# When the first FFN's weight sums are copied and added, and which engine rounds attention's first weights

## The chip, the cores and the metric

The kernel runs on one core of a Trainium2 chip. The time is the device time of one execution in microseconds (us). The engines are TensorE (PE in the profile; PEld is its weight load), VectorE (DVE), ScalarE (ACT), GpSimd (POOL) and SyncE (SP, which here only issues transfers). The core has 16 DMA engines; SP's transfers go through the queue that the profile calls hardware_dynamic (q1), GpSimd's through software_dynamic (q0).

## The reference

Two sequences, of 512 and 256 tokens with 16 learned tokens ahead of each (800 rows in all), go through a trunk of two layers: a bidirectional mLSTM mixer and a SwiGLU FFN, then differential attention and a SwiGLU FFN. All in float32.

```python
for i in range(DEPTH):                                   # DEPTH = 2
    xn = rmsnorm(h, norm_mix[i])
    h = h + (mlstm_mixer(xn, ...) if i % 2 == 0 else diff_attn(xn, ...))
    xn = rmsnorm(h, norm_ffn[i])
    gu = xn @ ffn_w_in[i]                                # 1024 -> 2 x 2816
    h = h + (silu(gu[..., :FF]) * gu[..., FF:]) @ ffn_w_out[i]
```

## The kernel before

**Float32 products.** TensorE multiplies rounded numbers. So each weight tile is loaded (`raw`, `raws`), rounded to a high part (`wh`, `w5h`), and the rest is taken as a low part (`wl`, `w5l`); a product is three matmuls per 128 rows of the weight: high by high, high by low, low by high.

**Blocks.** In the mixers a block is 128 output columns of a weight of 1024 rows: a tile of 512 KB, 48 matmuls (for 800 rows in two halves). Blocks are numbered: mLSTM's input projection has 24 (0 to 23), its output projection OUT0 = 24 to 31, attention's begin with MIX1 = 32. There are two slots. GpSimd's `split` (L715 to 727) does both steps: four casts (L722), four subtractions (L726). It waits until block n-1 is done, and SP's `weights` (L576) loads block n once split n-2 is done. Ahead of the output projection's third block SP also brings half of h back from DRAM (`h_kept`, L667).

**The FFN's jobs.** Each FFN is computed with seven products instead of eight (Strassen's scheme), so some factors are sums of weight quarters. An FFN has 42 jobs s: 22 are tiles of the first matrix ("input jobs", 12 matmuls per product), 20 of the second (6, in the last group 9). Each job has seven products j = 0 to 6, and `product_order` interleaves them into one list `ORDER` of 294 products, n = 0 to 293. Jobs 0 to 4, 9 to 12, 17 to 20 are input jobs; 5 to 8, 13 to 16 and so on are output jobs, run in between or alternating with an input job's products. The places of product 0 of some jobs: job 1 n = 7, 2 n = 14, 5 n = 33, 6 n = 38, 7 n = 46, 8 n = 53, 10 n = 70, 11 n = 77, 13 n = 89, 14 n = 94, 15 n = 102, 16 n = 109, 17 n = 115, 28 n = 196.

For each product n, SP loads the factor (`factor`, L603, DMA at L625: 256 KB for an input job, 128 KB for an output job), ScalarE rounds it (`high_part`, L2141 is its activation), GpSimd subtracts (`low_parts`, L756), TensorE multiplies (`product`, L922). There are seven raw buffers and five slots: load n waits for split n-7, rounding n waits for product n-5. All in program order on each engine; on ScalarE the rounding stands between copies of products (L2156), silu and roundings of the hidden factors.

**The weight sums.** The four sums of weight quarters that the scheme needs are made in DRAM by DMA. Each FFN's are cut into six parts of four copies and four adds, so there are 24 copies (`copy_for_sum`, L601, on SP's queue, 1280 or 1536 KB each) and 24 adds (`add_for_sum`, L738, L742, L748, accumulating transfers on GpSimd's queue, same sizes). An add waits for the copies of its part; the second kind of add waits for the first. Before the change, layer 0's copies 0 to 21 are issued with the blocks of mLSTM's input projection and 22, 23 with OUT0 and OUT0+1; its adds n-9 after split n for n = 9 to 31, and the last, add 23, in the FFN after split 14. Layer 1's copies are issued in the first FFN, one at product 0 of each of the jobs 10 to 33, its adds in attention.

Jobs 28 and up read the sums of layer 0's last two parts (copies and adds 16 to 23).

**From the FFN into attention.** The last products are 289 to 293. GpSimd then waits for product 290 (`prod_done` NF-3), splits block MIX1 (L722, L726), and TensorE's first attention block (L1329) follows product 293. Block MIX1's raw tile is loaded from 935 us on. ScalarE and VectorE meanwhile make `xh`, `xl` and squares of the last rows (L2282, L2285, L1542, L1549), then the root of the norm (L2126) and its reciprocal (L1422).

Of the kernel before, what the change touches and what calls it, by code (L numbers as in the profile page):

```python
# [21 lines left out]
F32 = mybir.dt.float32  # L22
F32R = mybir.dt.float32r
ALU = mybir.AluOpType
ACT = mybir.ActivationFunctionType
AX = mybir.AxisListType

P = 128
D = 1024
KT = D // P  # L30
# [4 lines left out]
KP = KT // 2  # L35
# [26 lines left out]
OUT0 = MIX0 + 6 * M_HEADS  # L62
MIX1 = OUT0 + KT
# [20 lines left out]
NPROD = 7  # L84
# [52 lines left out]
NF = len(ORDER)  # L137
# [31 lines left out]
N_SLOT, N_RAW = 5, 7  # L169
# [4 lines left out]
OUT_PARTS = ((0, 6), (6, 11))  # L174
PARTS = (("in", 0), ("in", 1), ("out", 0), ("in", 2), ("in", 3), ("out", 1))
N_PART = len(PARTS)


FX_POS = {B11: 1, T1: 2, B22: 3, T2: 4, T3: 5, B21: 6, T4: 7}
# [72 lines left out]
def trunk(nc, x_prompt, x_sample, meta_tokens, norm_mix, norm_ffn, m_w_in, m_b_gate, m_g_head, m_w_out,  # L252
# [3 lines left out]
    with ctx:  # L256
# [11 lines left out]
        raw = sb("raw", [P, 2, KT * P])  # L268
        wh, wl = sb("wh", [P, 2, KT * P], F32R), sb("wl", [P, 2, KT * P], F32R)
# [212 lines left out]
        raw_in = [sem("raw_in0"), sem("raw_in1")]  # L482
# [92 lines left out]
        def _(sp):  # L575
# [18 lines left out]
            def copy_for_sum(layer, i):  # L594

                part, which = divmod(i, 4)
                unit = N_PART * layer + part
                if which == 0 and unit > 1:
                    sp.wait_ge(sums_copied[unit % 2], 64 * (unit // 2))
                row, col = ((1, 0), (0, 0), (0, 0), (0, 1))[which]  # L600
                sp.dma_start(sum_columns(layer, (0, 2, 1, 3)[which], part),  # L601
                             weight_columns(layer, row, col, part)).then_inc(sums_copied[unit % 2], 16)
# [25 lines left out]
            def ffn_factors(layer):  # L628
                for n, (s, j) in enumerate(ORDER):
                    factor(layer, n)  # L630
                    if layer == 0 and j == 0 and 10 <= s < 34:
                        copy_for_sum(1, s - 10)

            def first_weights(j):
# [18 lines left out]
            for hd in range(1, M_HEADS):  # L653
                for j in range(6):
                    n = MIX0 + hd * 6 + j
                    weights(n, j % 2, mlstm_cols(hd, j))
                    if hd == 1 and j < 4:
                        copy_for_sum(0, 2 * j)
                        copy_for_sum(0, 2 * j + 1)
                    else:  # L660
                        copy_for_sum(0, n - 2)
            for j in range(2):
                weights(OUT0 + j, j, cols(m_w_out[0], j * P))
                copy_for_sum(0, OUT0 + j - 2)
            sp.wait_ge(pv_done, M_HEADS * NT)
            sp.wait_ge(h_stored, 16)
            sp.dma_start(h[:, KP:KT, :], h_kept).then_inc(h_back, 16)  # L667
# [29 lines left out]
        def _(pool):  # L697
# [18 lines left out]
            def split(n, slot, times, wait=True, k=KT):  # L716
                if wait:
                    pool.wait_ge(block_done, n - 1)
                pool.wait_ge(raw_in[slot], 16 * times)
                pool.sem_inc(pool_passed, 1)  # L720
                for c in pieces(k * P):
                    ins = pool.tensor_copy(wh[:, slot, c], raw[:, slot, c])  # L722
                ins.then_inc(w_hi, 1)
                pool.wait_ge(w_hi, n + 1)
                for c in pieces(k * P):
                    ins = pool.tensor_tensor(wl[:, slot, c], raw[:, slot, c], wh[:, slot, c].bitcast(F32), ALU.subtract)  # L726
                ins.then_inc(w_split, 1)


            def add_for_sum(layer, i):  # L730

                pair, step = divmod(i, 8)
                part = 2 * pair + ((step // 2) if step < 4 else step % 2)
                unit = N_PART * layer + part
                if step < 4:
                    pool.wait_ge(sums_copied[unit % 2], 64 * (unit // 2 + 1))
                    which, other = ((0, weight_columns(layer, 1, 1, part)), (2, weight_columns(layer, 1, 0, part)))[step % 2]
                    pool.dma_start(sum_columns(layer, which, part), other,  # L738
                                   accum_op=ALU.add).then_inc(sums_added[unit % 2], 16)
                elif step < 6:  # L740
                    pool.wait_ge(sums_added[unit % 2], 32 * (unit // 2 + 1))
                    pool.dma_start(sum_columns(layer, 1, part), sum_columns(layer, 0, part),  # L742
                                   accum_op=ALU.add).then_inc(sums_second[unit % 2], 16)
                else:
                    pool.wait_ge(sums_second[unit % 2], 16 * (unit // 2 + 1))
                    if unit > 1:
                        pool.wait_ge(sums_fourth[unit % 2], 16 * (unit // 2))
                    pool.dma_start(sum_columns(layer, 3, part), sum_columns(layer, 1, part),  # L748
                                   accum_op=ALU.add).then_inc(sums_fourth[unit % 2], 16)

            def low_parts(layer):
                for n, (s, j) in enumerate(ORDER):
                    pool.wait_ge(prod_hi, NF * layer + n + 1)
                    columns = k_tiles_of(s) * P
                    for c in pieces(columns):
                        ins = pool.tensor_tensor(slot_of(n, 1)[:, c], raw_of(n)[:, c], slot_of(n, 0)[:, c].bitcast(F32),  # L756
                                                 ALU.subtract)
                    ins.then_inc(prod_split, 1)
                    if layer == 0 and n == 2 * NPROD:
                        add_for_sum(0, 23)  # L760

            split(0, 0, 1, wait=False)
            pool.wait_ge(xl_ready, KT - 1)
            split(1, 1, 1, wait=False)
            for n in range(2, MIX1):
                split(n, n % 2, n // 2 + 1)
                if n >= 9:
                    add_for_sum(0, n - 9)
            low_parts(0)
            def split_rest(q):  # L770

# [10 lines left out]
                ins.then_inc(w_split, 1)  # L782

            pool.wait_ge(prod_done, NF - 3)
            split(MIX1, 0, MIX1 // 2 + 1)
            for x in (at[:, :, :, :], va[:, :, :, :]):
                pool.memset(x, 0.0).then_inc(attn_zeroed, 1)
            pool.wait_ge(prod_done, NF)
# [1327 lines left out]
        def _(sc):  # L2116
# [176 lines left out]
            def ffn(layer):  # L2293
                w, f0 = WIDTH[layer], layer * FT

                def silu(f):
                    gate = gate_up(layer, f)[0]
                    sc.wait_ge(g_ready, f0 + f + 1)
                    sc.activation(gate[:, 0:2 * w], gate[:, 0:2 * w], ACT.Silu).then_inc(silu_ready, 1)

                copied, finished = 0, 0
                for n in range(3, NF):
                    s, j = ORDER[n]
                    f = TILE_OF.get(s)
                    if f is not None and j < 3:
                        product_copy(layer, f, j)
                    if n + N_SLOT < NF:
                        high_part(layer, n + N_SLOT)
                    if n == 5:
                        root(2 * layer + 2)  # L2310
                    if f == 1:
                        if j == 0:
                            silu(0)
                        elif j < 3:
                            high_of_pair(layer, 0, (B11, T1)[j - 1])
                    elif f and f % 2 and j < 2:
                        high_of_pair(layer, f // 2, (B11, T1)[j])
                    elif f and f % 2 == 0 and j < 3:
                        for which in ((B22, T2), (T3, B21), (T4,))[j]:
                            high_of_pair(layer, f // 2 - 1, which)  # L2320
                    if f and j == 5:
                        silu(f)
                    if f == FT - 1 and j == 6:
                        for which in (B22, T2, T3, B21, T4):
                            high_of_pair(layer, f // 2, which)
                        if layer == 0:
                            rope_loads()
                    if layer == 0 and finished < KT and PLACE[LAST_TILES[finished]] + 1 <= n:
                        high_and_square(finished)
                        finished += 1  # L2330
                    while layer == 1 and copied < len(LAST_HALVES) and PLACE[LAST_HALVES[copied]] + 3 <= n:
                        copy_result(copied)
                        copied += 1
                if layer == 0:
                    lambda_loads()
                    for i in range(finished, KT):
                        high_and_square(i)
                    sc.wait_ge(lam_sums, 2)
                    sc.activation(lam[:, 4:6], lam[:, 0:2], ACT.Exp).then_inc(lam_exp, 1)
                    root(3)  # L2340
                else:
                    for t in range(copied, len(LAST_HALVES)):
                        copy_result(t)
# [292 lines left out]
```

## Time and profile before

| | |
|---|---|
| median of 3 runs | 1909.01 us (1906.89 to 1911.67) |
| the profiled execution | 1908.87 us, span 1907.0 us, mean granted clock 0.998 |
| TensorE busy | 1880.2 us (99% of the span) |
| VectorE, ScalarE, GpSimd busy | 65%, 46%, 61% |
| DMA | 305.39 MB, mean 160 GB/s; q1 40.6%, q0 20.0% of the 16 engines' span |
| chain that ended last | TensorE 89%, VectorE 6%, DMA 2% |

The span is the time from the first to the last instruction; the time of the runs has about 2 us around it. Times inside it are counted from its start. Stages: mLSTM's input projection and cells to 359 us, its output projection to 440, the first FFN to 948, attention to about 1417, the second FFN to the end. The granted clock is TensorE's, as a share of 2.4 GHz.

### The profile page before, as it was taken

How to read it: one execution, taken by the hardware profiler on the slowest of the kernel's cores; microseconds unless marked ns; L12 is line 12 of the kernel's file. 1: busy time of each engine (PE TensorE's matmuls, PEld its weight loads, DVE VectorE, ACT ScalarE, POOL GpSimd, SP SyncE). 2: the span in 40 equal slices, each digit the busy share in tenths (PEclk: the TensorE clock that was granted, in tenths of full speed). 3: DMA queues.
4: the chain of work that ended last, by engine and by line, in shares of the span. 5: the costliest groups of instructions: out<-in, count | busy, mean ns of one | idle time of the engine just before them, and what ended most of it. 6: DMA issues, size and time to landing. Idle time of an engine off the chain costs nothing.

```text
span 1907.0 us, 31586 instructions
## 1 busy us (share of the span) xinstructions
PE 1880.2 (99%) x10881; PEld 1750.9 (92%) x10881; DVE 1241.4 (65%) x2148; ACT 870.1 (46%) x1837; POOL 1165.7 (61%) x1537
## 2 busy tenths in 40 slices
PE   8999999999999999999999999999999999999999
PEld 7888887899999999999988888888889999999998
DVE  7756465667757565656776666666488575756673
ACT  6333333335544444445524444444465454544453
POOL 4533524376877777788853333333358787887885
PEclk9999999999999999999999999999999999999999
DMA  5559999697466978763366666656124435353534
GB/s 164 183 194 258 231 257 240 172 198 171 114 204 214 281 219 273 225 184 108 113 137 127 128 122 125 126 116 117 57 84 122 133 111 150 97 153 103 153 115 129
DMA packets 378985, 305.39 MB, mean 160 GB/s; under 512 B 14259, under 2 KB 322262, under 8 KB 378598
## 3 DMA queue, kind: packets, MB, share of 16 engines
q1 hardware_dynamic: 348304, 233.69, 40.6%
q0 software_dynamic: 28416, 69.21, 20.0%
q8 instruction: 73, 1.20, 0.3%
q10 hardware_dynamic: 2134, 0.82, 0.2%
q14 instruction: 58, 0.48, 0.1%
HBM read 298.88 MB, written 143.20 MB: 232 GB/s over the span
## 4 chain that ended last, share of the span: by engine, by line
PE 89%; DVE 6%; DMA 2%; ACT 1%; issue 1%; POOL 1%; ACTq 0%; DVEq 0%; SPq 0%; POOLq 0%
PE ps L922 50%; PE ps L829 24%; PE ps L1075 3%; PE ps L1236 3%; PE ps L1204 2%; DMA raw<-in_m_w_out_dram 2%; PE ps L1055 1%; PE ps L1226 1%; PE ps L1138 1%; POOL wl L726 1%; DVE rstd L1422 1%; DVE sx L1474 0%; PE ps L1168 0%; PE ps L1329 0%; PE ps L1040 0%
## 5 line engine op out<-in xcount | busy, mean ns | idle before, releaser
L922 PE MATMUL ps<-sx,wh 128*128 128x400 f32 (+1 forms) x2044 | 530.3, 340 | 0.9 <-POOL wl L756 0.5
L756 POOL TENSOR_TENSOR wl<-raw,wh 128x256 fp32r<-128x256 f32 (+1 forms) x432 | 352.5, 840 | 100.1 <-ACT wh L2141 98.7
L722 POOL CAST wh<-raw 128x256 fp32r<-128x256 f32 x252 | 105.2, 465 | 492.4 <-PE ps L829 443.8
L922 PEld LDWEIGHTS ps<-sx,wh 128*128 128x128 f32 x2044 | 373.4, 188 | 2.7 <-ACT gt_first L2156 0.9
L922 PE MATMUL ps<-sx,wl 128*128 128x400 f32 (+1 forms) x1022 | 347.6, 340 | 0.0
L756 POOL TENSOR_TENSOR wl<-raws,wh 128x256 fp32r<-128x256 f32 x328 | 285.2, 890 | 85.8 <-ACT wh L2141 84.8
L1633 DVE TENSOR_TENSOR h<-h,ps 128x400 f32<-128x400 f32 (+1 forms) x280 | 154.6, 559 | 132.5 <-PE ps L922 132.4
L922 PE MATMUL ps<-fx,wh 128*128 128x400 f32 (+1 forms) x904 | 235.3, 341 | 0.1
L829 PE MATMUL ps<-xh,wh 128*128 128x512 f32 (+1 forms) x752 | 215.9, 363 | 0.0
L829 PE MATMUL ps<-xl,wh 128*128 128x512 f32 (+1 forms) x752 | 207.4, 349 | 0.0
L726 POOL TENSOR_TENSOR wl<-raw,wh 128x256 fp32r<-128x256 f32 x252 | 198.9, 817 | 5.2
L829 PE MATMUL ps<-xh,wl 128*128 128x512 f32 (+1 forms) x752 | 201.3, 345 | 0.0
L922 PEld LDWEIGHTS ps<-sx,wl 128*128 128x128 f32 x1022 | 191.9, 188 | 0.0
L2141 ACT ACTIVATE wh<-raw 128x512 fp32r<-128x512 f32 (+2 forms) x268 | 142.4, 535 | 101.2 <-PE ps L922 93.2
L2141 ACT ACTIVATE wh<-raws 128x512 fp32r<-128x512 f32 (+2 forms) x202 | 108.5, 537 | 163.8 <-PE ps L922 155.8
L922 PEld LDWEIGHTS ps<-fx,wh 128*128 128x128 f32 x904 | 164.6, 188 | 0.5 <-issue 0.5
L922 PE MATMUL ps<-fx,wl 128*128 128x400 f32 (+1 forms) x452 | 153.7, 340 | 0.0
L922 PE MATMUL ps<-sx,w5h 128*128 128x400 f32 (+1 forms) x532 | 138.4, 341 | 0.3 <-ACT gt L2156 0.3
L829 PEld LDWEIGHTS ps<-xh,wh 128*128 128x128 f32 x752 | 120.8, 189 | 18.4 <-issue 7.4
L829 PEld LDWEIGHTS ps<-xl,wh 128*128 128x128 f32 x752 | 126.2, 188 | 10.5
L829 PEld LDWEIGHTS ps<-xh,wl 128*128 128x128 f32 x752 | 124.5, 188 | 10.8
L756 POOL TENSOR_TENSOR w5l<-raw,w5h 128x256 fp32r<-128x256 f32 x112 | 92.4, 841 | 21.7 <-ACT w5h L2141 21.5
(309 smaller groups left out, 3588.4 us busy)
## 6 DMA issues: line engine op xcount, KB each, us to landing
in_sums<-in_ffn_w_in_dram SPq DMA_DIRECT2D x16, 1536.0 KB, 9.2
raw<-in_sums SPq DMA_DIRECT2D x96, 256.0 KB, 3.0
in_sums<-in_ffn_w_in_dram SPq DMA_DIRECT2D x16, 1280.0 KB, 8.2
raw<-in_ffn_w_in_dram SPq DMA_DIRECT2D x80, 256.0 KB, 3.0
raws<-in_sums SPq DMA_DIRECT2D x80, 256.0 KB, 3.0
raw<-out_sums SPq DMA_DIRECT2D x120, 128.0 KB, 2.4
raws<-in_ffn_w_in_dram SPq DMA_DIRECT2D x52, 256.0 KB, 3.1
raw<-in_m_w_in_dram SPq DMA_DIRECT2D x24, 512.0 KB, 4.6
```

The costliest lines, as they stand in the source:

```text
L722: ins = pool.tensor_copy(wh[:, slot, c], raw[:, slot, c])
L726: ins = pool.tensor_tensor(wl[:, slot, c], raw[:, slot, c], wh[:, slot, c].bitcast(F32), ALU.subtract)
L756: ins = pool.tensor_tensor(slot_of(n, 1)[:, c], raw_of(n)[:, c], slot_of(n, 0)[:, c].bitcast(F32), ALU.subtract)
L829: mm = pe.matmul(out, w[:, slot, k * P:(k + 1) * P], x[:, k, a:b], start=(k + q == 0), stop=(k == k_tiles - 1 and q == 2), skip_group_chec ...
L922: mm = pe.matmul(product_bank(layer, s, j), slot_of(n, low_w)[:, k * P:(k + 1) * P], x, start=(j in OPENS and k + q == 0), stop=(k == tile ...
L1055: mm = pe.matmul(flat(2 + 0)[0:tz, (j % 2) * 1024 + a:(j % 2) * 1024 + b], wk[:, 1, t0:t0 + tz], wk[:, 0, START[s] + a:START[s] + b], star ...
L1075: mm = pe.matmul(ps[0:tz, 4 + 2 * (i % 2) + d, 0:M_DV + 2], w, v, start=(j == js[0] and t == 0), stop=(j == js[-1] and t == 2), skip_group ...
L1138: mm = pe.matmul(square_sums[0:lhs.shape[1], 2 * i:2 * i + 2], lhs, cst[:, COMP:COMP + 2], start=True, stop=True, skip_group_check=True)
L1204: return pe.matmul(both[:, c, a:b], wk[rows, odd, i * P:(i + 1) * P], wk[rows, 2 + odd, START[s] + a:START[s] + b], start=True, stop=True)
L1236: mm = pe.matmul(acc_o, at[:, i % 2, q, :], va[:, odd, j, :], start=(q == 0), stop=(j == js[-1]), skip_group_check=True)
L1633: ve.tensor_tensor(part, part, product_bank(layer, s, j), ALU.add if result_of(s, j)[0] >= 4 else ALU.subtract).then_inc(out_read, 1)
L2141: sc.activation(slot_of(n, 0)[:, 0:columns], raw_of(n)[:, 0:columns], ACT.Copy).then_inc(prod_hi, 1)
```

## The change

Layer 0's copies 16 to 23 are no longer issued with blocks 18 to 25 but in the first FFN, at product 0 of the jobs 1 to 8. Its adds 16 to 23 are no longer issued after splits 25 to 31 and in the FFN after split 14, but in the FFN after the split of product 0 of the jobs 6, 7, 10, 11, 13, 14, 16 and 17. Add 15 stays after split 24.

ScalarE makes the high part of block MIX1: one half after product 289, the other after product 290, in its own order of the FFN's work. GpSimd no longer casts there: it waits for both halves and subtracts. It also no longer waits for the raw tile or for an earlier block itself.

```diff
+LATE_ADDS = (6, 7, 10, 11, 13, 14, 16, 17)
...
                 for n, (s, j) in enumerate(ORDER):
                     factor(layer, n)
-                    if layer == 0 and j == 0 and 10 <= s < 34:
+                    if layer == 0 and j == 0 and 1 <= s < 9:
+                        copy_for_sum(0, s + 15)
+                    elif layer == 0 and j == 0 and 10 <= s < 34:
                         copy_for_sum(1, s - 10)
...
-                    else:
+                    elif n < 18:
                         copy_for_sum(0, n - 2)
             for j in range(2):
                 weights(OUT0 + j, j, cols(m_w_out[0], j * P))
-                copy_for_sum(0, OUT0 + j - 2)
...
                     ins.then_inc(prod_split, 1)
-                    if layer == 0 and n == 2 * NPROD:
-                        add_for_sum(0, 23)
+                    if layer == 0 and j == 0 and s in LATE_ADDS:
+                        add_for_sum(0, 16 + LATE_ADDS.index(s))
...
-                if n >= 9:
+                if 9 <= n < 25:
                     add_for_sum(0, n - 9)
...
             pool.wait_ge(prod_done, NF - 3)
-            split(MIX1, 0, MIX1 // 2 + 1)
+            pool.wait_ge(w_hi, MIX1 + 1)
+            for c in pieces(KT * P):
+                ins = pool.tensor_tensor(wl[:, 0, c], raw[:, 0, c], wh[:, 0, c].bitcast(F32), ALU.subtract)
+            ins.then_inc(w_split, 1)
...
                     if n + N_SLOT < NF:
                         high_part(layer, n + N_SLOT)
+                    elif layer == 0 and n >= NF - N_SLOT and n < NF - N_SLOT + 2:
+                        part = slice(KP * P, KT * P) if n == NF - N_SLOT else slice(0, KP * P)
+                        sc.wait_ge(prod_done, n + 1)
+                        sc.wait_ge(raw_in[0], 16 * (MIX1 // 2 + 1))
+                        ins = sc.activation(wh[:, 0, part], raw[:, 0, part], ACT.Copy)
+                        if n > NF - N_SLOT:
+                            ins.then_inc(w_hi, 1)
```

## Rows read from the trace of the kernel before

**Rows 1.** The chain that ended last, whole span: start us, us, what.

```profile
359.41 16.11 DMA raw<-in_m_w_out_dram
...
397.46 13.39 DMA raw<-in_m_w_out_dram
...
486.15 456.94 PE ps L922 x2505
```

**Rows 2.** TensorE in order, 355 to 417: start us, us, operation, [idle before <-releaser].

```profile
381.32 0.63 PE L829 MATMUL ps<-yh,wh 128*128 128x400 f32 x2 [1.84 <-POOL wl L726]
...
411.67 0.62 PE L829 MATMUL ps<-yh,wh 128*128 128x400 f32 x2 [2.23 <-POOL wl L726]
```

**Rows 3.** Busy time by engine (PE, PEld, DVE, ACT, POOL), clock, DMA share, GB/s.

```profile
381.00:386.00 5.00, 4.68 (x17) 4.69 (x18) 4.46 (x4) 2.43 (x5) 4.92 (x9) 0.66 0.73 167
```

**Rows 4.** DMA issues of 387.8 to 388.2: queue, count, KB each, us to landing.

```profile
out_sums<-in_ffn_w_out_dram POOLq DMA_DIRECT2D x1, 1280.0 KB, 15.2
raw<-in_m_w_out_dram SPq DMA_DIRECT2D x1, 512.0 KB, 17.7
```

**Rows 5.** DMA issues of 381.0 to 381.5.

```profile
raw<-in_m_w_out_dram SPq DMA_DIRECT2D x1, 512.0 KB, 4.2
```

**Rows 6.** DMA issues of 359 to 360.

```profile
h<-h_kept SPq DMA_DIRECT2D x1, 1600.0 KB, 7.7
```

**Rows 7.** All engines in order, 940 to 962.

```profile
943.28 1.92 POOL L722 CAST wh<-raw 128x256 fp32r<-128x256 f32 x4 [1.69 <-PE ps L922]
...
945.24 1.62 DVE L1542 SCALAR_TENSOR_TENSOR xl<-h,par,xh 128x800 fp32r<-128x800 f32 x1
...
945.27 4.30 POOL L726 TENSOR_TENSOR wl<-raw,wh 128x256 fp32r<-128x256 f32 x4
...
949.63 0.63 PE L1329 MATMUL ps<-xh,wh 128*128 128x400 f32 x2 [1.62 <-POOL wl L726]
...
959.88 0.15 DVE L1536 TENSOR_SCALAR lam<-lam 128x1 f32<-128x1 f32 x1
...
960.99 5.15 DVE L1422 RECIPROCAL rstd<-rstd 128x800 f32<-128x800 f32 x1 [0.95 <-ACT rstd L2126]
```

**Rows 8.** The first FFN's matmuls (L922): PE, PEld busy (count), clock, DMA share, GB/s.

```profile
439.60:640.00 200.40, 198.96 (x1084) 197.32 (x1085) 1.00 0.64 185
```

**Rows 9.** SP, GpSimd and TensorE in order, 516 to 534.

```profile
516.15 3.64 SPq L625 DMA_DIRECT2D raws<-in_ffn_w_out_dram  x3
516.48 0.74 POOL L756 TENSOR_TENSOR wl<-raws,wh 128x256 fp32r<-128x256 f32 x1 [0.36 <-ACT wh L2141]
...
522.30 3.54 SPq L625 DMA_DIRECT2D raw<-out_sums  x4
...
528.49 0.74 POOL L756 TENSOR_TENSOR wl<-raw,wh 128x256 fp32r<-128x256 f32 x1 [0.35 <-ACT wh L2141]
...
532.16 0.53 PE L922 MATMUL ps<-fx,wh 128*128 128x400 f32 x2
```

**Rows 10.** DMA issues of 621.3 to 621.6.

```profile
in_sums<-in_ffn_w_in_dram SPq DMA_DIRECT2D x1, 1536.0 KB, 7.5
raw<-out_sums SPq DMA_DIRECT2D x1, 128.0 KB, 7.2
```

**Rows 11.** Busy time by engine as in Rows 3, in the first FFN.

```profile
600.00:660.00 60.00, 60.00 (x331) 60.00 (x330) 33.95 (x53) 26.20 (x56) 43.42 (x55) 1.00 0.90 279
```

**Rows 12.** DMA queues in 434 to 440, an add beside loads: packets, MB, share.

```profile
q0 software_dynamic: 356, 1.09, 93.5%
q1 hardware_dynamic: 358, 0.18, 15.2%
```

**Rows 13.** The same in 280 to 288, an add beside a copy.

```profile
q1 hardware_dynamic: 393, 1.21, 41.4%
```

**Rows 14.** DMA issues of 192.7 to 193.4, issued beside an add.

```profile
in_sums<-in_ffn_w_in_dram SPq DMA_DIRECT2D x1, 1280.0 KB, 13.9
```

**Rows 15.** SP in order, 608 to 630.

```profile
627.62 0.98 SPq L625 DMA_DIRECT2D raws<-in_ffn_w_out_dram  x1
```

## The prediction

> **What bounds the kernel now.** I read the page first, then the chain that ended last, then the stretch around each place that the change touches. On the page TensorE is busy for nearly the whole span, so time can come only from the few places where it idles, and a new place where it idles costs in full. The chain [rows 1] shows both kinds. In the mLSTM's output projection it runs twice through a transfer, `raw<-in_m_w_out_dram`, 16.11 and 13.39 us. In the first FFN it is one piece of 2505 matmuls, 456.94 us, with nothing between: there TensorE waits for nobody.
>
> A chain piece of 16.11 us is not a gap of 16.11 us. In the order of TensorE's instructions [rows 2] it idles 1.84 us ahead of block OUT0+2 (381.32) and 2.23 us ahead of OUT0+5 (411.67), both times for GpSimd's split, which waited for the load. Behind the first gap the granted clock is 0.66 over 5 us [rows 3]: TensorE works part of it at the lower level (1.2 GHz) after it idled, which costs (1 - 0.66) x 5 = 1.7 us. I take the same behind the second. So late loads cost the projection 1.84 + 2.23 + 2 x 1.65 = 7.4 us.
>
> Why they are late: the 512 KB load for OUT0+5 took 17.7 us while an add of GpSimd's queue (15.2 us) flew [rows 4]; one issued together with an add, whose packets had not begun, took 4.2 [rows 5].
>
> **The change, part by part.**
>
> *Output projection.* Adds 16 to 22 leave the seven splits from OUT0+1 on, copies 16 to 23 leave SP's queue in head 3 and at OUT0 and OUT0+1. What is left beside the weights is the reload of h, 7.7 us [rows 6], with the load of OUT0+2 behind it: together at most 7.7 + 4.2 = 12 us from 359.4, so it lands by 371.4 and is split by 377 (5.5 us as in the old rows), before TensorE wants it at 379.5. Both gaps and both slow stretches go: -7.4 us. Bounds: 0 to -7.4, for behind each gap stand only TensorE's own matmuls; I take the whole, since the adds are gone altogether. GpSimd also issues seven DMAs fewer between splits (no gain, it waits for TensorE there). What follows up to 486 us hangs on TensorE, ScalarE and VectorE and slides forward whole.
>
> *ScalarE's rounding.* At the FFN's end GpSimd starts four casts at 943.28, when product 290 is done, and four subtractions at 945.27 that take 4.30 us; TensorE waits 1.62 us, until 949.63 [rows 7]. In the new kernel ScalarE rounds one half after product 289 and the other after 290, ahead of the xh copy that stands there. A rounding takes about half a us (my estimate; GpSimd's four casts took 1.92), so the xh copy moves by about 1 us, and VectorE's operation that reads it starts only at 945.24 [rows 7]: nobody behind it is late. The subtractions start at about 943.8, 1.5 us earlier, and end at 948.1 at the latest; TensorE comes at 948.0. Its gap goes. But VectorE's reciprocal, the chain's next piece (960.99), stands behind VectorE's small operations, the last of which ends at 960.03 [rows 7]: it can move by 0.95 us and no more. I take -0.9 (bounds 0 and -1.6).
>
> *First FFN: what comes in.* Eight copies (jobs 1 to 8) and eight adds (jobs 6, 7, 10, 11, 13, 14, 16, 17, at product 0 of each) instead of the one add at product 14. Each product's factor is loaded, rounded by ScalarE, split by GpSimd, and SP issues load n+7 when split n ends. So the question is how long a load may take. TensorE is 1084 matmuls into the FFN at 640.0 [rows 8], at 331 in 60 us; product 47 (job 6, factor 4) has 492 ahead of it, so it is the one that starts at 532.16 [rows 9]. Its load is the first of the four issued from 522.30, its split runs from 528.49 to 529.23 [rows 9], behind 0.5 us of ScalarE. A load there may take 532.16 - 522.30 - 1.35 = 8.5 us before TensorE stands. Where a copy stands ahead of a load in SP's queue, the load takes 7.2 us already (copy 7.5) [rows 10]: the copies that are there now use nearly all of the slack, and TensorE loses nothing. The way from load to product is nine products of 6 matmuls. Where products have 12, in the input jobs, it is 9 x 2.18 = 19.6 us, less 2.2 for the longer split: 17 us.
>
> The eight copies alone I cost at 0: same sizes, same place in the queue as those from job 10 on, under which TensorE is busy 60.00 us of 60 at a DMA share of 0.90 [rows 11]. From above, one late load each in jobs 5 to 8: 2 us.
>
> The adds are another matter. While an add flies, the two queues move packet for packet: 356 and 358 beside loads in 6 us [rows 12], 60 per us; beside a copy 393 in 8 us [rows 13], 49 per us. A copy beside an add took 13.9 us [rows 14]. An add or copy is 512 packets of 2.5 or 3 KB, or 640 of 2 KB; a 128 KB load is 256 of 512 B. A copy alone moves about 150 per us (from its 7.5 us, less some 3.5 of start and end: an estimate).
>
> The Trainium skill says the same (DMA: Bandwidth & Descriptors, "Queues, rings and completion order"): each DMA engine takes the queues that have work in turn, one packet of each. By that rule a load's small packets go at the pace of the add's large ones; if the engines were shared by bytes, the loads would lose only half their rate and the sum would be rival 1's. The trace agrees with turn-taking (356 to 358).
>
> Three places, in the times of the profiled run:
> - A, jobs 6 and 7. Split 38 (516.48) ends at 517.2, its add's packets flow from about 520. Load 46, the third of those from 516.15 [rows 9], takes till 524.3. Copy 22 (640 packets, behind it) moves 226 beside the rest of the add, to 529, 300 alone until the next add, issued just ahead of split 47, flows at 531, and the last 114 beside that, to 533.2. Load 47 needs 256 / 60 = 4.3 us more and lands at 537.8, split at 539.1; TensorE has waited since 532.2: **7 us**.
> - B, jobs 13 to 15, two adds 9 us apart. Products of 12 and of 6 matmuls alternate, so the way is half as long again as in A, and only one copy falls in: **3 us**, an estimate between 0 and A's.
> - C, jobs 16 and 17. Add 22 is issued with load 116 (627.62 [rows 15]), the copy of layer 1 just ahead of them. That copy takes 512 / 49 = 10.4 us from 630.4, to 641; load 116 lands at 642, load 117 (512 packets) goes beside add 23 at 80 per us (2 KB packets), to 648. Product 117 has 1086 matmuls ahead, so it starts at 640.4 and wants its load by 638: **10 us**.
>
> The adds at jobs 10 and 11 meet input jobs alone, 14 us of latency where 17 are free: 0. Behind each of the three waits TensorE works at the lower clock: 3 x 1.65 = 5. Sum 25 us. Bounds: below, 0 if the waits don't come; above, about 45 if ScalarE, held by a late load, also brings its product copies and silu late, so that banks come free late. GpSimd's own waits in the adds are met long before, and the first job that reads these sums is the 28th.
>
> **Sum.** -7.4 - 0.9 + 25 = +16.7 us. The profiled execution took 1908.87 us (span 1907.0); the median is 1909.01, 0.01% above. Forecast: 1926 us.
>
> **Rivals.**
> 1. The FFN absorbs it. For: with copies alone it loses nothing, and four products are split ahead. Against: A comes to 537.8 - 522.3 = 15.5 us of latency where 8.5 are free, and the projection shows 17.7 [rows 4]. 1908.9 - 8.3 = 1900.6. Chance 0.18.
> 2. Only one of the places bites and cancels the gain: 1904 to 1912. Chance 0.10.
> 3. Heavier: each late load holds ScalarE's queue, five or six waits come, each with its slow clock. For: ScalarE rounds in order, with product copies behind. Against: it is busy only 26.20 of 60 us [rows 11] and catches up. 1908.9 - 8.3 + 45 = 1946. Chance 0.19.
> 4. The reload of h alone keeps the projection's first gap: 3.7 us less gain, 1930. Chance 0.05.
>
> The sign turns where a load behind a copy and beside an add takes more than about 8.5 us.
>
> **Chances.** Forecast 0.48. Over 0.3% (6 us) is what a measurement of this kernel can tell from no change. Faster: 0.18 of rival 1 and 0.01 of 2, 0.19. Same: 0.06, of rival 2. Slower: 0.75, the rest. Range 1900 to 1944: down to rival 1, without the upper half of rival 3. The forecast's own range is 1918 to 1938.
>
> **What would show it.** No `raw<-in_m_w_out_dram` in the chain and no granted clock under 1 in the output projection; TensorE no longer idle ahead of L1329's first matmul. In the first FFN, idle stretches of TensorE for GpSimd's split with a load behind it near products 47, 98 to 103 and 116 to 117, a lower clock after them, and ScalarE waiting for a DMA over 5 us at a time. If TensorE is busy 60 of 60 us through jobs 5 to 18, the packet-for-packet reckoning of late loads failed, and the forecast with it.

## The result, and the profile after

The changed kernel takes 1933.22 us (median of 4 runs, 1931.89 to 1934.96), the kernel before, in the same session, 1910.34 us (4 runs, 1906.89 to 1913.50): ratio 1.0121, 95% interval 1.0107 to 1.0135. It is 23 us slower. The profiled execution took 1933.13 us, its span is 1931.3 and its mean granted clock 0.991, where the kernel before had 1907.0 and 0.998. Ratios, here and below, are of the mean times; medians are given beside them.

Line numbers are 4 to 7 higher in the new kernel: the FFN's matmuls are L929, GpSimd's low part L760, ScalarE's high part L2148 and, for MIX1, L2320, the mixers' blocks L836 and L1336, a split's casts L726 and subtractions L730, VectorE's reciprocal L1429.

Chain of waits, whole span (start us, us, what):

```profile
375.75 3.83 POOL wl L730 x4
379.71 52.90 PE ps L836 x288
...
514.11 11.23 DMA raw<-out_sums
526.68 12.84 DMA raw<-out_sums
...
582.74 13.86 DMA raw<-in_sums
...
621.35 13.12 DMA raw<-out_sums
635.82 5.54 DMA raw<-out_sums
642.71 19.69 DMA raw<-in_sums
664.74 270.37 PE ps L929 x1470
```

This stands against [rows 1]. The two transfers are gone from the output projection, which is one piece of 288 matmuls; the one piece in the first FFN is broken by transfers of weights down to 664.74.

TensorE's instructions in order, against [rows 2]: the only one in the output projection (360 to 432) that came after idle time, then all those between 520 and 670:

```profile
379.71 0.63 PE L836 MATMUL ps<-yh,wh 128*128 128x400 f32 x2 [0.19 <-POOL wl L730]
...
526.79 1.00 PE L929 MATMUL ps<-fx,wh 128*128 128x400 f32 x2 [2.67 <-POOL wl L760]
540.97 1.00 PE L929 MATMUL ps<-fx,wh 128*128 128x400 f32 x2 [4.98 <-POOL wl L760]
615.43 0.63 PE L929 MATMUL ps<-sx,wh 128*128 128x400 f32 x2 [0.58 <-DVE ut L1573]
623.33 0.60 PE L929 MATMUL ps<-fx,wh 128*128 128x400 f32 x2 [1.09 <-POOL wl L760]
626.57 0.60 PE L929 MATMUL ps<-fx,wh 128*128 128x400 f32 x2 [1.90 <-POOL wl L760]
629.84 1.00 PE L929 MATMUL ps<-fx,wh 128*128 128x400 f32 x2 [1.95 <-POOL wl L760]
657.44 1.01 PE L929 MATMUL ps<-fx,w5h 128*128 128x400 f32 x2 [5.13 <-POOL w5l L760]
664.74 1.01 PE L929 MATMUL ps<-sx,wh 128*128 128x400 f32 x2 [4.96 <-POOL wl L760]
```

The first row is the start of the projection's third block, where [rows 2] has 1.84 us; the stop of 2.23 us has no successor. The other eight are products 47, 54, 92, 97, 98, 99, 116 and 117: 23.3 us. Seven of them wait for GpSimd's split; the one of 0.58 us, product 92, waits for VectorE (`ut`).

Busy time by engine, clock, DMA share, GB/s, first in the stretch of [rows 3], then behind the second and last waits:

```profile
381.00:386.00 5.00, 5.00 (x29) 5.00 (x28) 4.06 (x5) 2.84 (x5) 4.13 (x5) 1.00 0.33 97
...
540.00:545.00 5.00, 4.03 (x12) 4.03 (x13) 0.57 (x1) 2.28 (x6) 4.42 (x7) 0.50 0.73 201
...
664.00:669.00 5.00, 4.26 (x13) 4.25 (x14) 0.93 (x2) 2.69 (x6) 3.34 (x5) 0.50 0.83 236
```

The output projection runs at the full clock. In the first FFN the granted clock falls to 0.50, the level of 1.2 GHz, behind the second and the last wait, and stays there for the whole of each stretch.

The FFN's matmuls from the first to the last, TensorE's busy time and then its weight loads', before (L922) and after (L929):

```profile
439.69:947.84 508.15, 506.79 (x2772) 504.72 (x2772) 1.00 0.65 192
```

```profile
432.45:974.78 542.33, 517.72 (x2772) 513.59 (x2772) 0.97 0.76 217
```

These two rows are the ledger. The FFN begins 439.69 - 432.45 = 7.24 us earlier and takes 34.18 us longer: idle time went from 1.36 to 24.61 us (+23.25), and the same 2772 matmuls are busy 10.93 us longer, at the lower clock. From the FFN's last matmul to the end of the span it takes 2.64 us less (959.16 to 956.52). 34.18 - 7.24 - 2.64 = +24.30, the difference of the spans.

How long the loads take is seen in the DMA issues of 514 to 519 and of 642.6 to 644.2 (queue, count, KB each, median us to landing), where the load of [rows 5] took 4.2 and that of [rows 10] 7.2:

```profile
raw<-out_sums SPq DMA_DIRECT2D x4, 128.0 KB, 10.0
```

```profile
raw<-in_sums SPq DMA_DIRECT2D x2, 256.0 KB, 20.9
raw<-out_sums SPq DMA_DIRECT2D x1, 128.0 KB, 22.1
```

And the two queues' packets, MB and share in 530 to 535, where an add flies (q0) beside a copy (q1), as in [rows 13]:

```profile
q0 software_dynamic: 245, 0.75, 77.2%
q1 hardware_dynamic: 245, 0.49, 29.3%
```

Packet for packet to the last one, 49 per us each, as in [rows 13]; beside loads [rows 12] showed 356 to 358.

At the FFN's end, all engines in order:

```profile
968.81 0.62 ACT L2320 ACTIVATE wh<-raw 128x512 fp32r<-128x512 f32 x1
...
970.05 0.63 ACT L2320 ACTIVATE wh<-raw 128x512 fp32r<-128x512 f32 x1 [0.62 <-PE ps L929]
...
970.83 3.59 POOL L791 TENSOR_TENSOR wl<-raw,wh 128x256 fp32r<-128x256 f32 x4 [2.30 <-ACT wh L2320]
...
974.78 0.53 PE L1336 MATMUL ps<-xh,wh 128*128 128x400 f32 x2
...
981.13 0.35 DVE L1535 CUSTOM_DVE_ANT_0 lv<-lv 128x64 f32<-128x64 f32 x1
...
986.06 5.15 DVE L1429 RECIPROCAL rstd<-rstd 128x800 f32<-128x800 f32 x1 [0.44 <-ACT rstd L2133]
```

L791 is the subtraction that the change writes out. It ends at 974.42, ahead of TensorE's need, and the idle 1.62 us of [rows 7] is gone.

### The profile page after: what moved, and what is told of

It reads as the page before. It is cut to its first block, busy times and chain, and to the rows that moved or that the text cites. A ratio compares the mean times of both kernels' runs of the same rounds, so it can differ in the third digit from the quotient of the medians.

```text
span 1931.3 us, 31585 instructions
## 1 busy us (share of the span) xinstructions
PE 1887.1 (98%) x10881; PEld 1756.6 (91%) x10881; DVE 1246.1 (65%) x2148; ACT 871.4 (45%) x1839; POOL 1161.5 (60%) x1533
## 4 chain that ended last, share of the span: by engine, by line
PE 85%; DVE 5%; DMA 4%; POOL 2%; ACT 2%; issue 1%; SPq 0%; ACTq 0%; DVEq 0%; POOLq 0%
PE ps L929 45%; PE ps L836 25%; PE ps L1082 3%; PE ps L1243 3%; PE ps L1211 2%; DMA raw<-out_sums 2%; DMA raw<-in_sums 2%; PE ps L1062 1%; POOL wl L760 1%; PE ps L1233 1%; PE ps L1145 1%; DVE rstd L1429 1%; PE ps L1091 1%; DVE sx L1481 0%; PE ps L1175 0%
## 5 line engine op out<-in xcount | busy, mean ns | idle before, releaser
L929 PE MATMUL ps<-sx,wh 128*128 128x400 f32 (+1 forms) x2044 | 531.7, 341 | 6.2 <-POOL wl L760 5.5
L760 POOL TENSOR_TENSOR wl<-raw,wh 128x256 fp32r<-128x256 f32 (+1 forms) x432 | 352.2, 842 | 123.5 <-ACT wh L2148 122.1
L726 POOL CAST wh<-raw 128x256 fp32r<-128x256 f32 x248 | 102.2, 454 | 488.9 <-PE ps L836 466.1
L929 PEld LDWEIGHTS ps<-sx,wh 128*128 128x128 f32 x2044 | 374.5, 188 | 8.0 <-issue 5.5
L929 PE MATMUL ps<-sx,wl 128*128 128x400 f32 (+1 forms) x1022 | 348.3, 341 | 0.0
L760 POOL TENSOR_TENSOR wl<-raws,wh 128x256 fp32r<-128x256 f32 x328 | 284.2, 895 | 81.7 <-ACT wh L2148 81.3
L929 PE MATMUL ps<-fx,wh 128*128 128x400 f32 (+1 forms) x904 | 239.9, 347 | 12.9 <-POOL wl L760 12.6
L836 PE MATMUL ps<-xh,wh 128*128 128x512 f32 (+1 forms) x752 | 215.5, 363 | 0.0
L836 PE MATMUL ps<-xl,wh 128*128 128x512 f32 (+1 forms) x752 | 207.4, 349 | 0.0
L2148 ACT ACTIVATE wh<-raw 128x512 fp32r<-128x512 f32 (+2 forms) x268 | 142.5, 535 | 132.0 <-PE ps L929 88.8
L836 PE MATMUL ps<-xh,wl 128*128 128x512 f32 (+1 forms) x752 | 201.3, 345 | 0.0
L730 POOL TENSOR_TENSOR wl<-raw,wh 128x256 fp32r<-128x256 f32 x248 | 196.7, 822 | 5.1
L929 PEld LDWEIGHTS ps<-sx,wl 128*128 128x128 f32 x1022 | 192.5, 188 | 0.0
L2148 ACT ACTIVATE wh<-raws 128x512 fp32r<-128x512 f32 (+2 forms) x202 | 108.5, 538 | 163.0 <-PE ps L929 150.5
L929 PEld LDWEIGHTS ps<-fx,wh 128*128 128x128 f32 x904 | 167.5, 192 | 15.1 <-issue 13.6
L929 PE MATMUL ps<-fx,wl 128*128 128x400 f32 (+1 forms) x452 | 155.6, 344 | 0.0
L929 PE MATMUL ps<-sx,w5h 128*128 128x400 f32 (+1 forms) x532 | 138.3, 341 | 0.3 <-ACT gt L2163 0.3
L836 PEld LDWEIGHTS ps<-xh,wh 128*128 128x128 f32 x752 | 120.8, 189 | 18.6 <-issue 7.4
L836 PEld LDWEIGHTS ps<-xl,wh 128*128 128x128 f32 x752 | 126.2, 188 | 10.3
L836 PEld LDWEIGHTS ps<-xh,wl 128*128 128x128 f32 x752 | 124.4, 188 | 10.8
L760 POOL TENSOR_TENSOR w5l<-raw,w5h 128x256 fp32r<-128x256 f32 x112 | 93.5, 856 | 22.9 <-ACT w5h L2148 22.7
## 6 DMA issues: line engine op xcount, KB each, us to landing
in_sums<-in_ffn_w_in_dram SPq DMA_DIRECT2D x16, 1280.0 KB, 10.3
```

Of the source, the lines that this page charges most:

```text
L836: mm = pe.matmul(out, w[:, slot, k * P:(k + 1) * P], x[:, k, a:b], start=(k + q == 0), stop=(k == k_tiles - 1 and q == 2), skip_group_chec ...
L929: mm = pe.matmul(product_bank(layer, s, j), slot_of(n, low_w)[:, k * P:(k + 1) * P], x, start=(j in OPENS and k + q == 0), stop=(k == tile ...
L2148: sc.activation(slot_of(n, 0)[:, 0:columns], raw_of(n)[:, 0:columns], ACT.Copy).then_inc(prod_hi, 1)
```

## The experiments

Each kernel is compared with the kernel before on the same chip and in the same session. The reference's median was 1910.34 beside the changed kernel and 1910.44, 1911.43 or 1910.82 in the three sessions below, so the sessions agree within 1.1 us.

**The rounding alone.** The kernel before with ScalarE's rounding of MIX1 and nothing else of the change.

```diff
-            split(MIX1, 0, MIX1 // 2 + 1)
+            pool.wait_ge(w_hi, MIX1 + 1)
+            (GpSimd's four subtractions, ScalarE's two roundings as in the change)
```

> The kernel before with ScalarE's rounding of attention's first block and nothing else. Forecast's step: TensorE's gap of 1.62 us ahead of L1329's first matmul goes, VectorE's reciprocal moves by 0.95 us at most: -0.9 us. Rival (the reciprocal moves the whole way, since VectorE's small operations slide too): -1.6 us. Rival (the rounding holds ScalarE's xh copy and the gap only changes hands): 0.

1906.04 us against 1910.44; ratio 0.9983 (0.9972 to 0.9994): by the ratio 3.2 us faster, between 1.1 and 5.3, by the medians 4.4. In the profile TensorE's wait ahead of its first attention block fell from 1.62 to 0.37 us, and the way from the FFN's end to the reciprocal from 13.15 to 11.92. That is 1.2 us, between the 0.9 of the forecast and the 1.6 of the first rival. Where the rest of the 3.2 comes from is not shown; the profiled execution was one of the slower (1908.93). It does show how executions of this program differ. The projection's second stop took 0.43 us instead of 2.23 and the FFN began 3.46 us earlier (436.23), and then TensorE stopped there, where the kernel before had no stop, with the granted clock at 0.66 behind it (443 to 448):

```profile
443.86 1.03 PE L925 MATMUL ps<-sx,wh 128*128 128x400 f32 x2 [3.10 <-ACT gt_first L2159]
```

ScalarE had waited 3.46 us for a weight load beside which an add flew.

**The adds' transfers cut away.** The changed kernel, with layer 0's adds 16 to 23 reduced to 16 columns of one row block. The kernel leaves the sums of the last two parts unfinished, so only its time is of use.

```diff
+                def cut(x):
+                    return x[:, 0:1, 0:16] if layer == 0 and i >= 16 else x
-                pool.dma_start(sum_columns(...), other, ...)
+                pool.dma_start(cut(sum_columns(...)), cut(other), ...)
```

> The kernel after, with layer 0's adds 16 to 23 cut to one 128-row tile by 16 columns each (so the last two parts' sums are left unfinished); all copies, waits and places as in the kernel after. Theory (the adds cost everything, the eight copies nothing): TensorE has no gap in the first FFN from product 20 on, and the gains of the output projection and of the rounding stay: 1901 us, -8 against before, -32 against after. Rival (the copies of jobs 5 to 8 are late by themselves): gaps at products 47 and 54 stay, 1906 to 1909 us.

1898.31 us (1897.82 to 1898.76); ratio to the kernel before 0.9938 (0.9919 to 0.9958). Its FFN, read as above:

```profile
432.65:939.85 507.20, 506.06 (x2772) 504.92 (x2772) 1.00 0.69 209
```

All eight waits and all the slow clock are gone, with the eight copies where the change put them. So the adds' transfers cost 1933.2 - 1898.3 = 34.9 us, and the copies by themselves nothing. It is also the price of everything else in the change: -12.1 us against its own reference, 1910.44, by the ratio between -8.0 and -15.5. The forecast had -8.3. The profiled executions differ by 10.3 (spans 1907.0 and 1896.7): 7.0 up to the FFN's start, 1.0 in the FFN, 2.3 behind it.

**One add, with and without a copy.** The kernel before, its add 23 moved from product 14 to product 46 (job 7, where no copy is near), and in a second kernel to product 109 (job 16, beside layer 1's copies).

```diff
-                    if layer == 0 and n == 2 * NPROD:
+                    if layer == 0 and (s, j) == (7, 0):      # second kernel: (16, 0)
                         add_for_sum(0, 23)
```

> The kernel before, with add 23 (640 packets of 2 KB) issued behind the split of product 46 (job 7, products of 6 matmuls) instead of product 14. No copy is in SP's queue there. Theory (loads and adds go packet for packet, and a load is late only where a copy stands ahead of it too): the add moves its packets for about 8 us, loads issued in it take 4 to 7 us where 8.5 are free, TensorE stays busy, 0 +- 2 us against before. Rival (any add among output jobs stalls TensorE, with or without a copy): a gap of 3 to 5 us near products 51 to 56 and a slow clock behind it, +5 us.

> The kernel before, with the same add 23 issued behind the split of product 109 (job 16), where one of layer 1's copies is issued at the same moment. Theory (copy and add share packet for packet, the copy takes 10 us instead of 4, the load behind it is late): TensorE idles 3 to 5 us at product 116 and works at the lower clock behind it, +5 us (4 to 7) against before. Rival (an add alone is what hurts): the same loss as in the kernel with the add at job 7. Rival (an add hurts only with a second add behind it): 0.

Job 7: 1910.19 us, ratio 0.9999 (0.9987 to 1.0011). Job 16: 1916.85 us, ratio 1.0036 (1.0023 to 1.0049). TensorE's stops in the first, and in the second:

```profile
538.71 0.60 PE L922 MATMUL ps<-fx,wh 128*128 128x400 f32 x2 [0.93 <-POOL wl L756]
```

```profile
641.95 1.00 PE L922 MATMUL ps<-fx,w5h 128*128 128x400 f32 x2 [3.29 <-POOL w5l L756]
645.52 1.00 PE L922 MATMUL ps<-sx,wh 128*128 128x400 f32 x2 [1.23 <-POOL wl L756]
```

The same transfer costs nothing in one place and 6.4 us in the other. The issues behind them, job 7 (525.8 to 530), then job 16 (628.9 to 630.4):

```profile
out_sums<-out_sums POOLq DMA_DIRECT2D x1, 1280.0 KB, 12.0
raw<-out_sums SPq DMA_DIRECT2D x3, 128.0 KB, 9.2
```

```profile
raw<-in_sums SPq DMA_DIRECT2D x2, 256.0 KB, 14.2
raw<-out_sums SPq DMA_DIRECT2D x1, 128.0 KB, 13.9
```

9.2 us is just over the 8.5 that the prediction gave an output job's load before TensorE stands, and the stop is just under 1 us. With a copy in front it is 14. The two kernels differ in more than the copy: two of the loads at job 16 are of 256 KB. One add at job 16 without layer 1's copies was not run; the copies alone are taken away further on, from the changed kernel.

**The copies back.** The changed kernel, copies 16 to 23 back beside blocks 18 to 25; adds as changed.

```diff
-                    if layer == 0 and j == 0 and 1 <= s < 9:
-                        copy_for_sum(0, s + 15)
...
+                copy_for_sum(0, OUT0 + j - 2)
```

> The kernel after, with layer 0's copies 16 to 23 back in head 3 and at OUT0 and OUT0+1; the adds stay at jobs 6 to 17. Theory (a load is late only behind a copy beside an add): at jobs 6 to 8 no copy is left, so the gaps at products 47 and 54 shrink from 8 us to at most 2 and their slow clock goes; those at jobs 12 to 17 stay, where layer 1's copies stand. 1923 us (1920 to 1926), -10 against after. Rival (adds one job apart are enough): 1931 to 1934.

1925.03 us, ratio 1.0073 (1.0055 to 1.0092), in the range that I expected. Place A, jobs 6 and 7, shrinks from 2.67 + 4.98 to one stop of 2.28 us at full clock, and the output projection still ends as early (FFN at 432.43): the adds were what delayed it, not the copies. B (products 99 and 100) has 1.91 + 1.21, and C is larger, 13.3 us against 10.1:

```profile
650.73 1.01 PE L928 MATMUL ps<-fx,w5h 128*128 128x400 f32 x2 [10.20 <-POOL w5l L759]
656.19 1.00 PE L928 MATMUL ps<-sx,wh 128*128 128x400 f32 x2 [3.12 <-POOL wl L759]
```

**Layer 1's copies later.** The changed kernel; the copies that fall beside B and C begin at job 18.

```diff
-                    elif layer == 0 and j == 0 and 10 <= s < 34:
-                        copy_for_sum(1, s - 10)
+                    elif layer == 0 and j == 0 and 18 <= s < 42:
+                        copy_for_sum(1, s - 18)
```

> The kernel after, with layer 1's 24 copies at jobs 18 to 41 instead of 10 to 33, so that no copy stands beside the adds of jobs 10 to 17. Theory: the gaps at 92 to 101 go; of those at 116 and 117 (10.6 us) some 5 us stay, since two adds follow each other there and load 117 is 512 packets long; those at 47 and 54 stay. 1922 us (1918 to 1926). Rival (the adds alone do it): 1931 to 1934.

1917.48 us, ratio 1.0030 (1.0019 to 1.0042), just below the range that I expected. A stays (2.19 and 6.02 us), B is gone, and C is down from 10.1 us to 1.84 + 2.15 (products 117 and 119). This is the cleanest evidence for the copy's part: the adds are the same and in the same places. It also shows that the copy is not all of it. Two adds that follow each other among output jobs still cost 4.0 us at C with no copy near, and 2.3 at A in the kernel above.

**The adds in input jobs.** The changed kernel; its adds at input jobs, where the prediction counted 17 us free.

```diff
-LATE_ADDS = (6, 7, 10, 11, 13, 14, 16, 17)
+LATE_ADDS = (10, 11, 12, 18, 19, 25, 26, 27)
```

> The kernel after, with the eight adds at jobs 10, 11, 12, 18, 19, 25, 26 and 27 (input jobs, products of 12 matmuls), copies as in the kernel after. Theory (a load may take 17 us there, beside a copy and an add it takes 14 to 16): most gaps go, 2 to 5 us stay where the products turn to 6 matmuls behind job 12. 1904 us (1900 to 1908), faster than before. Rival (each add costs what it cost, 4 us, wherever it is): 1931 us.

1911.14 us, ratio 1.0001 (0.9990 to 1.0013). 22 us back against the changed kernel, but 7 short of what I expected, which was a kernel faster than before; it is level with it. Two stops are left, 3.88 us at product 88 and 3.27 at product 186, and they are of another kind. TensorE's waits (engine, line, waited for: us, times, longest), TensorE's and ScalarE's order at the first of them:

```profile
PE ps L929 <- ACT gt L2163: 7.4, 3, 3.9
```

```profile
598.66 0.63 ACT L2148 ACTIVATE wh<-raw 128x512 fp32r<-128x512 f32 x1 [4.92 <-DMA raw<-in_sums]
...
600.04 0.48 ACT L2163 ACTIVATE gt<-ps 128x400 f32<-128x400 f32 x1
```

```profile
600.58 1.03 PE L929 MATMUL ps<-sx,wh 128*128 128x400 f32 x2 [3.88 <-ACT gt L2163]
```

TensorE has its weights. It waits for a bank, which ScalarE empties (L2163), and ScalarE stood 4.92 us in front of a rounding whose load took 13.3 us. The bound on a load is here where ScalarE's program meets it, not where TensorE needs it: 13.3 - 3.9 = 9.4 us were free, an estimate from this one stop. This is the mechanism of rival 3, at a small part of its price. It does not strike at every such load: in the changed kernel the load issued at 582.74, at job 12, took 13.9 us,

```profile
raw<-in_sums SPq DMA_DIRECT2D x1, 256.0 KB, 13.9
```

ScalarE waited 4.82 us for it, and TensorE did not stop: the next copy of a product in ScalarE's order (L2163, at 601.77) had itself to wait 1.35 us for TensorE.

**Adds and copies apart.** Both together: `LATE_ADDS = (4, 9, 10, 11, 12, 17, 18, 19)`, and layer 1's copies from job 18.

> The kernel after, with the adds at jobs 4, 9, 10, 11, 12, 17, 18 and 19 and layer 1's copies at jobs 18 to 41, so that adds and copies hardly meet. Theory: no gap in the first FFN from product 20 on; the output projection's and the rounding's gains are kept, 1899 us (1897 to 1902), as with the adds cut short. Rival (24 bytes-heavy adds anywhere in the FFN cost some us each): over 1905.

1903.08 us (1901.01 to 1907.90), ratio 0.9952 (0.9935 to 0.9968): faster than both kernels, 4 us above what I expected. The profiled execution is the slowest of the four (1907.90), so its stops are more than the median's. At jobs 10 to 12, where no copy flies, it has one stop of 1.11 us, again for ScalarE's L2163; at 17 to 19, where copies of layer 1 fly again from job 18 on, three of 1.05, 0.94 and 2.53 us.

**No add beside a copy.** Copies 16 to 23 as before the change, adds in the first input jobs, layer 1's copies from job 18.

```diff
+LATE_ADDS = (1, 2, 3, 4, 9, 10, 11, 12)
```

> The changed kernel with three places moved: layer 0's copies 16 to 23 back beside blocks 18 to 25 and the output projection's first two, its adds 16 to 23 at product 0 of jobs 1, 2, 3, 4, 9, 10, 11 and 12 (all input jobs), layer 1's copies from job 18 on. So in the first FFN no add flies beside any copy. If a load is late only where a copy stands ahead of it and an add beside it (my theory), no gap of TensorE follows any of the eight adds but for at most 1 us each at jobs 9 to 12, where output jobs' last loads or two products in turn are near, and the time is near that with the adds cut away: 1899 us, 1897 to 1903. Rival: an add beside 256 KB loads alone costs too, since a load of 512 packets at 60 to 80 per us takes 7 to 9 us and ScalarE's queue is held, as adds_and_copies_apart showed at product 72 (1.3 us): then 1903 to 1908, with gaps behind each of the adds.

1901.40 us (7 runs, 1901.00 to 1902.56), ratio 0.9960 (0.9945 to 0.9974). Its FFN:

```profile
432.50:942.86 510.36, 507.82 (x2772) 504.25 (x2772) 1.00 0.75 209
```

This is inside the 1897 to 1903 that I expected. Eight whole adds in the first FFN cost 3 us here (1901.4 against 1898.3 with the adds cut away), where the change paid 34.9, and the granted clock is 1.00 over the FFN. Of the rival's gaps behind each add only one is near its size, 0.96 us at product 72. Three things differ from the changed kernel at once: no copy is near an add, the adds stand at input jobs, and most of them are further apart. How the 32 us divide among the three is not shown. GpSimd's time for issuing an add, 1.2 to 1.5 us, is paid here too, so it is not by itself what stopped TensorE. Like the kernel before it in this section it beats both the old and the changed one; the intervals of the two overlap, so neither is shown to be the better.

## Why the prediction was right

The forecast was 1926 us and slower; it is 1933.2, inside the forecast's own range of 1918 to 1938. The mechanism held in all three places: loads behind a copy and beside an add came late, and ScalarE waited for transfers up to 6.2 us at a time. The sizes within a place held less well.

- **Output projection, -7.4.** -7.24, and nothing idles over 0.2 us in it. Rival 4 (the reload of h keeps the first gap) is out: the reload took 6.7 us and the load of OUT0+2, forecast by 371.4, landed at 369.1.
- **ScalarE's rounding, -0.9.** TensorE's gap went, as forecast. The cap did not hold: I took VectorE's small operations to end 0.95 us ahead of the reciprocal whatever happens, but the first of them had waited 1.73 us for its own transfer in the old trace (`lv`, at 955.62), and no longer does. From the FFN's end to the reciprocal it takes 1.87 us less, to the end of the span 2.64; the last 0.8 is not traced. The forecast took a wait for a load as fixed work.
- **The eight copies, 0.** Shown by the kernel with the adds cut away.
- **Add beside copy.** A was forecast at 7 us and took 7.7, B at 3 (0.6 + 1.1 + 1.9 + 2.0 = 5.5), C at 10 (10.1): 20 forecast, 23.3 measured. Moving layer 1's copies took away B and most of C, moving layer 0's most of A, and the two kernels with one add agree; what stays without a copy, 2.3 to 4.0 us, was seen only where two adds follow each other. That A came out so close is in part luck. The forecast had load 47 take 15.5 us and product 47 wait 7; the load took 11.2 and the product waited 2.67. The other 4.98 us are at product 54, whose load took 12.8 us and which the forecast left out. B was an estimate between 0 and A's, and 0.58 of its 5.5 us waits for VectorE, not for a split.
- **Slow clock, 5.** The term that was mis-sized: 10.9. I counted three waits, there were five long enough to be followed by the level of 1.2 GHz (2.67, 4.98, 1.95, 5.13, 4.96), and 10.9 / 5 is 2.2 us for each, not 1.65. This one term, 5.9 us too small, is most of the 7 us between forecast and result; the waits add 3.3, and the 1.7 more that was gained behind the FFN goes the other way.
- **Adds at jobs 10 and 11, 0.** Right: 14 us of latency were forecast and 13.9 measured, with no stop. But the 17 us of slack in input jobs do not hold everywhere. The kernel with its adds in input jobs stopped TensorE for 3.88 us behind a load of 13.3, because ScalarE's order came into it.
- **Turn-taking.** 245 to 245 packets in 5 us. The 80 per us that the forecast took for an add of 2 KB packets show as 243 in 3 us in the kernel with the add at job 7. What the reckoning lacked is the start: a load issued while an add flies moves nothing at first. In the kernel with the add at job 7, the first of four loads is issued at 528.11, and in 528 to 531 the queues show:

```profile
q0 software_dynamic: 208, 0.43, 98.9%
```

and there is no row for q1. From 532 to 535 the two are level again, 243 and 223. These 3 us are a large part of why a load beside an add alone takes 9.2 us and not the 256 / 60 = 4.3 of its packets.

Rival 1 (absorbed) had nearly the right time for the change without its adds, 1900.6 against 1898.3, but the adds were not absorbed. Rival 3's five or six late loads came, seven of them by the stops, but not its cause: each of the changed kernel's seven large stops waits for GpSimd's split, a late operand, and none for a bank.

## What to carry to other kernels

A background transfer costs by what flies beside it and by the slack where it flies: the same eight adds cost 34.9 us in one placement and 3 in another. Look for the places where an accumulating transfer of one queue meets a large copy standing ahead of small loads in the other, or a second add right behind it, and keep them apart before giving up either. Read the slack of a load at the first engine whose program order meets it, here ScalarE, and at what stands behind it there, not at the engine that finally needs the data. And when a forecast has waits of TensorE in it, price the clock behind the long ones too: here it came to 2.2 us for each of five.

## What the runs showed of the hardware

- In the changed kernel each stop of TensorE of 1.95 us or more was followed by matmuls at 1.2 GHz (1.00 us for two instead of 0.60), those of 0.58 to 1.90 us were not. Over all the runs the stops of 2.67 us and more in the first FFN (up to 10.20) were each followed by a granted clock of 0.50 to 0.66. Shorter ones went both ways. 1.84 us in [rows 2] was followed by 0.66; 1.21 us in the kernel with the copies back, which came 1.3 us of work after a stop of 1.91, by 0.50; but 2.28 us in that same kernel by 1.00, and so was 2.53 us in the kernel with adds and copies apart, in the stretch behind it, 682 to 687:

```profile
682.00:687.00 5.00, 5.00 (x29) 5.00 (x29) 2.11 (x4) 1.89 (x4) 3.93 (x7) 1.00 1.08 304
```

  So the length of one stop does not decide it alone.
- The kernel before varies by 9 us from run to run (1904.8 to 1914.1 in the experiments' sessions). With the adds cut away it varies by 1 us (1897.82 to 1898.76, 4 runs), with no add beside a copy by 1.6 (1901.00 to 1902.56, 7 runs), but with adds and copies apart by 6.9 (1901.01 to 1907.90, 4 runs). The stops in the projection vary too while the adds stand there: the second took 0.43 us in one profiled execution and 2.23 to 2.68 in three others, with the same program up to that point. That adds beside weight loads make the spread is my reading of it; no run varied that alone.
- Loads issued as an add's packets began to flow moved none for 3 us (208 packets of the add and none of the loads, 528 to 531 in the kernel with the add at job 7), and then went one for one, 243 to 223.
- The Trainium skill (DMA: Bandwidth & Descriptors, "Queues, rings and completion order") says that a DMA engine goes round the queue rows that have work, a packet of each; the trace agrees once both queues move, 245 to 245. Why one queue moved nothing in the 3 us before that, no run here shows.
